# Two transformer blocks on one core: TensorE's operands at other addresses, panel 0 on another queue, splits moved

## The reference

```python
# first_block: two layers; what a part returns is normed too before it is added
h = h + rmsnorm(gmlp_mixer(rmsnorm(h)))        # layer 0
h = h + rmsnorm(diff_attention(rmsnorm(h)))    # layer 1
h = h + rmsnorm(conv_ffn(rmsnorm(h)))          # after the mixer of either layer, 1024 -> 2 x 2816 -> 1024
# second_block: one layer
x = x + 0.5 * swiglu(rms_norm(x))
u = rms_norm(x) @ w_in
x = x + concat([mla_attention(...), moba_attention(...)]) @ w_out
x = x + 0.5 * swiglu(rms_norm(x))
return rms_norm(x, final_norm)
```

## Time and profile before

| | us |
|---|---|
| median of 3 runs | 1079.1 (1078.93 to 1079.15) |
| the profiled execution | 1078.41 |
| its span, first to last instruction | 1076.5 |
| TensorE busy | 1064.8 |
| VectorE busy | 773.5 |
| ScalarE busy | 653.1 |

### The profile page before, as it was taken

The page is one execution under the profiler, slowest core; times in us unless marked ns, Lnnn a source line. Parts: engine busy times, 40 slices in busy tenths (PEclk is TensorE's granted clock), DMA queues, the critical chain, the costliest instruction groups (busy, mean ns, idle before and its releaser), DMA issues.

```text
span 1076.5 us, 15631 instructions
## 1 busy us (share of the span) xinstructions
PE 1064.8 (99%) x5976; PEld 910.5 (85%) x5976; DVE 773.5 (72%) x1213; ACT 653.1 (61%) x1176; POOL 35.5 (3%) x39
## 2 busy tenths in 40 slices
PE   8999999999999999999999999999999999999997
PEld 7988888888799878888888888888899878888886
DVE  5888977878767889777788655665676857565554
ACT  5767766557757777566667545545566647454453
POOL 0830000000000000000000000000000000000000
PEclk9999999999999999999999999999999999999999
DMA  9763866566463347555554755556355516565651
GB/s 349 257 209 128 249 201 199 187 189 202 164 223 112 111 161 243 187 200 187 182 190 146 234 198 186 176 192 219 122 174 156 196 59 206 186 183 192 194 174 40
DMA packets 56777, 198.13 MB, mean 184 GB/s; under 512 B 6576, under 2 KB 8536, under 8 KB 56704
## 3 DMA queue, kind: packets, MB, share of 16 engines
q1 hardware_dynamic: 56016, 195.89, 55.6%
q10 hardware_dynamic: 576, 1.05, 0.3%
q0 software_dynamic: 112, 0.20, 0.1%
HBM read 195.35 MB, written 1.25 MB: 183 GB/s over the span
## 4 chain that ended last, share of the span: by engine, by line
PE 95%; ACT 2%; DVE 2%; DMA 1%; issue 0%; ACTq 0%
PE G L1407 28%; PE Y L1487 27%; PE G L1411 14%; PE G L1392 3%; PE G L1393 3%; PE G L1394 3%; PE G L1442 2%; PE G L1443 2%; PE G L1448 2%; PE Y L1482 2%; PE Y L1393 1%; PE Y L1392 1%; PE Y L1394 1%; PE G L1461 1%; PE G L1615 1%; PE Y L1495 1%
## 5 line engine op out<-in xcount | busy, mean ns | idle before, releaser
L868 DVE TENSOR_TENSOR w_low<-raw,w_high 128x1024 fp32r<-128x1024 f32 x352 | 425.0, 1225 | 37.6 <-ACT w_high L448 36.0
L448 ACT CAST w_high<-raw 128x1024 fp32r<-128x1024 f32 x352 | 363.5, 1045 | 12.0 <-DMA raw<-in_panels 8.4
L1407 PE MATMUL G<-x_parts,w_high 128*128 128x512 f32 x1280 | 325.3, 396 | 0.0
L1407 PEld LDWEIGHTS G<-x_parts,w_high 128*128 128x128 f32 x1280 | 233.4, 188 | 49.6
L537 ACT COPY big<-G 128x512 f32<-128x512 f32 x80 | 46.9, 586 | 246.5 <-PE G L1411 246.5
L1411 PEld LDWEIGHTS G<-x_parts,w_low 128*128 128x128 f32 x1280 | 172.9, 188 | 14.6
L962 DVE TENSOR_TENSOR w<-G,big 128x512 f32<-128x512 f32 x80 | 55.3, 691 | 172.2 <-ACT big L537 172.2
L1411 PE MATMUL G<-x_parts,w_low 128*128 128x256 f32 x1280 | 175.9, 280 | 0.0
L1487 PE MATMUL Y<-w_high,a_high 128*128 128x512 f32 x420 | 133.8, 400 | 0.0
L1487 PE MATMUL Y<-w_high,a_low 128*128 128x512 f32 x420 | 132.2, 396 | 0.0
L1487 PE MATMUL Y<-w_low,a_high 128*128 128x512 f32 x420 | 132.0, 395 | 0.0
(11 more groups left out here) (256 smaller groups left out, 1204.0 us busy)
## 6 DMA issues: line engine op xcount, KB each, us to landing
raw<-in_panels SPq DMA_DIRECT2D x351, 512.0 KB, 4.3
gain_pre<-in_gains SPq DMA_DIRECT2D x7, 512.0 KB, 5.7
gain_post<-in_gains SPq DMA_DIRECT2D x4, 512.0 KB, 6.4
big<-in_xT SPq DMA_DIRECT2D x4, 256.0 KB, 7.0
h<-in_x SPq DMA_DIRECT2D x2, 512.0 KB, 6.8
big<-rel_rows SPq DMA_DIRECT2D x8, 128.0 KB, 4.9
raw<-in_panels ACTq DMA_DIRECT2D x1, 512.0 KB, 5.2
big<-in_w_s SPq DMA_DIRECT2D x1, 512.0 KB, 9.2
```

The costliest lines, as they stand in the source:

```text
L448: s.copy(WH[:, n % RING, :], raw[:, n % RAWS, :]).then_inc(hi, 1)
L868: v.tensor_tensor(WL[:, n % RING, :], raw[:, n % RAWS, :], WH[:, n % RING, :].bitcast(F32), ALU.subtract).then_inc(lo, 1)
L1407: mm(out, WH[:, n % RING, k * P:(k + 1) * P], X2[:, k, :, :], start=k == 0, stop=False, skip_group_check=True)
```

## The change

1. An unused tensor `lead` of 1920 bytes comes first, and `x_parts`, `a_high`, `a_low` and the two `c4` tensors are declared before `h`. `raw`, `w_high`, `w_low`, `x_parts`, `a_high`, `a_low` and `c4_high` then start at multiples of 2 KB, `c4_low` 1 KB above one. `h` and `big2` get wider, with the same contents.
2. Panel 0 is loaded by SyncE, after the first piece of xT, and no longer by ScalarE, whose first transfer is now that of the gains `g`.
3. In MIX, the cast of panel B + 19 moves behind `turned_out(9, 0)`, and its subtraction behind `low_out(8)`. The cast of B + 35 moves behind the last `cast`, and the subtractions of B + 34 and B + 35 move behind `low_out(15)` and into `boundary(6)`.

```diff
@@ -100,20 +100,22 @@
         def sem(name):
             return ctx.enter_context(nc.semaphore(name))
 
+
+        sb("lead", [P, 480])
         raw = sb("raw", [P, RAWS, W])
         WH = sb("w_high", [P, RING, W], F32R)
         WL = sb("w_low", [P, RING, W], F32R)
-
-        h = sb("h", [P, TT, D + 2])
         X2 = sb("x_parts", [P, KT, 2, T], F32R)
         AH = sb("a_high", [P, KT, T], F32R)
         AL = sb("a_low", [P, KT, T], F32R)
         c4h = sb("c4_high", [P, T], F32R)
         c4l = sb("c4_low", [P, T], F32R)
+
+        h = sb("h", [P, TT, D + 16])
         gP = sb("gain_post", [P, D])
         gN = sb("gain_pre", [P, D])
         big1 = sb("big1", [P, 2048])
-        big2 = sb("big2", [P, 2052])
+        big2 = sb("big2", [P, 2048 + 32])
         big3 = sb("big3", [P, HEADS * SC])
         w3 = sb("w3", [P, 3, 2 * 2 * SC])
         qk = sb("qk", [P, 2, 2, T])
@@ -162,7 +164,7 @@
         sg = big1[:].rearrange("p (k t) -> p k t", k=KT)
         u8 = big2[:, 0:2048].rearrange("p (k t) -> p k t", k=KT)
         xT = big2[:, 0:2048].rearrange("p (k t) -> p k t", k=KT)
-        sqj = big2[:].rearrange("p (t d) -> p t d", t=TT)
+        sqj = big2[:, 0:TT * (D + 2)].rearrange("p (t d) -> p t d", t=TT)
         lows = big2[:, 0:4 * T].rearrange("p (f m t) -> p f m t", f=2, m=2)
         first2 = big1[:, 0:2 * 512].rearrange("p (t c) -> p t c", t=TT)
         wsT = big3[:, 0:D]
@@ -331,7 +333,7 @@
                 sp.dma_start(xT[:, 2 * q:2 * q + 2, :], io["xT"][:, 2 * q:2 * q + 2, :]).then_inc(xt_in[q], 16)
 
             x_part(0)
-            load(1)
+            load(0), load(1)
             x_part(1)
             load(2), load(3)
             x_part(2), x_part(3)
@@ -632,7 +634,6 @@
                 s.activation(qk[:, a % 2, 0, :], bank[:, 0:T], ACT.Copy, scale=DIFF_D ** -0.5)
                 s.copy(qk[:, a % 2, 1, :], bank[:, T:2 * T]).then_inc(qk_r, 1)
 
-            act.dma_start(raw[:, 0, :], io["panels"][0]).then_inc(ld[0], 16)
             act.dma_start(g0[:], io["gain_first"]).then_inc(g0_in, 16)
             act.wait_ge(consts, 1)
 
@@ -814,10 +815,12 @@
             upto(B + 17)
             qk_out(9)
             turned_out(8, 0), turned_out(8, 1)
-            upto(B + 19)
+            upto(B + 18)
             exps(9)
             qk_out(10)
-            turned_out(9, 0), turned_out(9, 1)
+            turned_out(9, 0)
+            upto(B + 19)
+            turned_out(9, 1)
             cast(8)
             upto(B + 21)
             exps(10)
@@ -839,7 +842,8 @@
             upto(B + 31)
             for a in range(12, 16):
                 turned_out(a, 0), turned_out(a, 1)
-                upto(B + 20 + a)
+                if a < 15:
+                    upto(B + 20 + a)
                 if a == 12:
                     exps(13)
                 elif a < 15:
@@ -1366,7 +1370,8 @@
             for a in range(12, 16):
                 if a < 15:
                     combine(a + 1)
-                upto(B + 20 + a)
+                if a < 14:
+                    upto(B + 20 + a)
                 outs(a)
                 if a > 12:
                     low_out(a - 1)
```

## The result

The changed kernel takes **1066.99 us** (median of 4 runs, 1066.69 to 1067.02); the kernel before took 1079.01 beside it (4 runs, 1078.76 to 1079.15). The ratio is 0.9888, 95% interval 0.9871 to 0.9905: 12.0 us faster. The forecast was 1075.3. The profiled execution took 1067.01 us, its span is 1065.1, and TensorE's granted clock is 0.999 on average.

A forecast was written before the change was run, and what follows sets the result against it. TensorE was taken as the bound, through its matmul pace and few pauses. Gains of 2.5 + 0.9 + 0.4 + 0 = 3.8 us took 1079.1 to 1075.3 us; the 8 in 10 range was 1067 to 1078.6.

The forecast's parts named there:

- What bounds the kernel: Whole kernel: TensorE, busy 99% of the span; only its matmul pace and the places where it stands can move the time.
- exchange rate: All matmuls: every 1 ns in 512 columns, with 0.5 in 256, is worth 3.2 us.
- Part 1, the start: First transfers: earlier g and panel 0 handling bring real work forward; gain 2.5 us, bounds 1.2 and 3.2.
- The smaller of the two gains named there: Start, up to panel 1: gain 2.4 us instead of 3.8.
- Part 2: Last two pairs of heads in the mixer: postponed splits end TensorE's standing before the last transposes; gain 0.9 us.
- part 3: Mixer, panel MIX+19: a later cast lets TensorE go earlier at 814.20; gain 0.4 us, bounds 0 and 0.5.
- Part 4, the addresses: Operand tensors moved to offset 0: no change of matmul pace, taken as 0 us.
- small form: Matmul stream: new addresses give 2 ns less for 512 columns, 1 less for 256, worth 6.4 us; chance 0.07.
- the addresses speed the stream: Rival on all matmuls: the new addresses quicken their pace; chances 0.05 and 0.07 for its two sizes.
- large form: Matmul stream: new addresses bring long matmuls to the lowest time they can come to; chance 0.05.
- The rival that slows it: Matmul stream: new addresses slow the pace; at 3 ns more, 1084.9 us; chance 0.08.

The follow-up runs named there:

- e2: The kernel before with only the new load, cast and subtraction order, operand addresses left as they were; 1075.40 us, ratio 0.9974.
- e3: The changed kernel with weights and activations all 128 bytes above a multiple of 2 KB; 1067.47 us.
- e6: The changed kernel with all TensorE operands 160 bytes above a multiple of 2 KB; 1067.05 us, one run.
- e4: The changed kernel with weights and activations all 1024 bytes above a multiple of 2 KB; 1066.98 us.
- e5: The changed kernel with x_parts, a_high, a_low and c4 64 bytes above a multiple of 2 KB, the weights at 0; 1069.90 us, one run.
- e11: The changed kernel with x_parts 64 bytes above the weights' offset, a_high and a_low equal to it; 1066.87 us, ratio 0.9892.
- e12: The changed kernel with x_parts at 64 and a_high, a_low at 192 bytes above the weights' offset; 1067.49 us, ratio 0.9898.
- e1: The kernel before with only the new addresses, old order and queues; 1070.25 us, ratio 0.9925.

## Why the prediction was wrong, step by step

**What bounds the kernel** was right: TensorE's pace decides, and the last part of the prediction said that 1 ns in 512 columns is worth as much as all the rest. 4.3 to 5.0 ns came, and were worth 14.0 us, less 5.2 that the 256-column matmuls gave back, where the prediction's exchange rate has them go along by half as much.

**Part 1, the start (2.5 us).** Right within 0.3 up to panel 7. `g` landed at 4.5 as taken, the first real matmul came at 6.74 (6.6 taken), panel 1 at 9.60 (9.4), without a fall of the clock. The smaller of the two gains named there, 2.4 us with the clock fallen, was the author's estimate, and no run shows it; in the trace of before, the one step of 512 columns wholly inside the stretch with a granted share of 0.50 took 0.43 us, from 10.32 to 10.75. ScalarE's cast of panel 7 moved by 0.36 us (at most 0.5), and TensorE's pause before it was 0.64 us more than a step (about 1). At panel 7 the gain is 2.8 us, in `e2` 2.6. What the step missed stands behind it: it followed TensorE only to the end of that stage, and in GMLP VectorE's `a_low` held it for 0.77 us in `e2` (0.16 in the changed kernel). It looked for slack at the later panels alone; the activations had about 0.9 us of it (`a_low` done near 60.8, used at 61.85 before), against 2.6 won.

**Part 2 (0.9 us) and part 3 (0.4 us).** Right as far as the trace goes. 0.99 us of standing became 0.09, and the uncovered 0.1 us in the chain of the second 128 tokens is too small to be seen. For part 3, TensorE's timeline at the scores of pair 10, of the kernel before (one row more than in the earlier trace rows) and of the changed one:

```profile
813.39 0.50 PE L1615 MATMUL G<-cst,w 128*128 128x128 f32 x3
```

```profile
805.73 0.50 PE L1620 MATMUL G<-cst,w 128*128 128x128 f32 x3
806.16 0.50 PE L1603 MATMUL Y<-qk 64*128 64x128 f32 x4
```

From the transposes to the scores of pair 10 it was 814.20 - 813.39 = 0.81 us and is 0.43: 0.38 us won. Neither part was run by itself; together with the start they gave 3.1 us in `e2`, for 3.8 predicted, and the difference is GMLP's wait.

**Part 4, the addresses (0): the step that failed.** It read two rows with a moving operand at 128 and one at 160, found 0.2334 us in both, and concluded: "I take 0, because that is what two different offsets agree on". The offsets differed, but each row was of a *pair*: 128 moving over 160, and 160 moving over 128. In both the two operands lay 32 bytes apart, and that was the condition that cost 4.5 ns. Rows that share a condition agree with each other and prove nothing about it. The rows were said to exclude "a price on 32, 64 or 128-byte alignment", and of one operand alone they did; `e3` and `e6` are as fast at 128 and 160 as at 0. Of the pair nothing was excluded.

**The rivals.** The small form of "the addresses speed the stream", at a chance of 0.07, was 2 ns less for 512 columns and 1 ns less for 256, worth 6.4 us at the 3.2 us for each ns that the prediction reads from the earlier trace rows, so 1068.9 us. It came near, in part by luck: it was 4.3 to 5.0 less and 1.7 to 2.9 *more*, which left 8.8. The large form, at 0.05, was the author's estimate; no run shows its term, the lowest that a long matmul can come to: the lowest mean of any kind of 512 columns was 227.9 ns, and no run took less than 1066.69 us. The rival that slows it had the sign wrong. In the kernel before, the offsets of the two operands of a matmul differed by 32 bytes, and D took 233.4 ns; where they are equal, as in the changed kernel, it takes 228.7. With 0.12 of the chance on both forms, the range ended at 1067, at the very place where the result came.

## What to carry to other kernels

Where matmuls of 512 columns start every 233 ns, as they did here before, look at the addresses of both operands of each kind of matmul *as a pair*, and try tensors whose starts differ by 0 or by 256 bytes, the two distances that gave 228.6 to 228.7 ns in D (the pieces of the tensors lie multiples of 512 apart). Equal offsets at 128, 160 and 1024 bytes above a multiple of 2 KB did as well as at 0 (`e3`, `e6`, `e4`: 1067.47, 1067.05 and 1066.98 us, against 1066.99), and `h`, 8,208 bytes long, between the weights and `x_parts` cost 8.3 of 1078.5 us. This is shown for matmuls of 512 columns in fp32r; those of 256 columns went the other way (u 117.2 to 118.9 ns, t 116.9 to 119.8). Before costing an edit at nothing because several rows agree, write down what all those rows have in common. And follow a gain at the start past the first stage: the step at which TensorE's lead met operands that VectorE had made took 0.77 us back in `e2` and 0.16 in the changed kernel.

## What the hardware showed that was not expected

- *Distance of the operands.* By how far the moving operand's tensor starts above the stationary one's, 512 columns took 227.9 to 229.1 ns at 0 and 256 bytes, 229.2 to 230.6 at 64 (U in `e5`, `e11`, `e12`; D in `e12`, where it is 64 less 256), 233.2 to 233.3 at -64, 233.1 to 233.4 at 32 and -32, and 232.0 to 233.2 at 128 and -128. So 64 bytes count differently in the two directions. Why is open: no matmul was measured by itself, and no run varied the distance in steps finer than these. One place speaks for the matmul's own stationary operand as the other of the pair, and not the one that is loaded next: when the last matmul of D before a tile of U starts, with `w_low` moving, the load of the tile's first piece of `w_high` starts too, and these two have the same offset in before and after. Yet the step took 234.3 ns before and 226.7 after (64 such steps in either trace).
- *Shorter matmuls go the other way.* With 256 columns the fast layouts are the slower ones: t took 119.8 ns at 0 and 116.9 at 32, u 118.9 and 117.2, 115.9 in `e5`. t mixes two pairs in `e11` and `e12`: with `x_parts` moving, 64 above w, it took 117.8 in `e5`, 117.5 and 117.3, and with `a_high` or `a_low` moving 119.5 in `e11`, at 0, and 113.8 in `e12`, at 192, the lowest of all (79 distances). But u took 115.9, 117.7 and 117.6 at one and the same distance of 64, so the pair alone doesn't set the pace. What else moves it wasn't found.
- *The start had two outcomes before.* The four runs of the changed kernel lie within 0.33 us. Of 11 runs of the kernel before, four with a mean granted clock of 0.998 took 1077.2 to 1077.4 us, and seven with 0.997 took 1078.5 to 1079.1. The profiled one is of the second kind, with the stretch at the lower level (granted share 0.50 for 2.94 us) in the earlier trace rows. No execution of the first kind was profiled, but `e1`, which has the same start, shows it without that stretch (columns of the earlier trace rows), and panel 1 began at 12.09 instead of 13.19:

```profile
8.03:10.97 2.94, 2.76 (x16) 2.27 (x17) 2.49 (x4) 2.94 (x6) 0.00 (x0) 1.00 1.04 413
```
